# Expert sums in banks of eight keys, neuron weights prepared later in each eight, and turned x tiles spread over the first row quarters

## The reference

```python
def peer(h, w_query, sub_keys, u_emb, v_emb):
    ...
    s_val, s_idx = lax.top_k(s, PEER_TOPK)
    cand = s_val[..., 0, :, None] + s_val[..., 1, None, :]
    ...
    gate = jax.nn.softmax(best, -1).astype(t.dtype)
    ...
        ub = jnp.take(u_emb, eb, axis=0)
        vb = jnp.take(v_emb, eb, axis=0)
        act = jax.nn.gelu(jnp.einsum('td,ted->te', tb, ub), approximate=False) * gb
        return jnp.einsum('te,ted->td', act, vb)
...
    x = x + ga2 * peer(modulate(rmsnorm(x, g_ffn[l]), sh2, sc2), w_query[l], sub_keys[l], u_emb[l], v_emb[l])
return rmsnorm(x, g_final)
```

## Time and profile before

| | |
|---|---|
| three runs | 3451.1, 3449.22, 3443.9 us; median 3449.22 |
| profiled execution | 3447.79 us, its span 3446.0 us |
| PE busy | 98% of the span |
| DVE, POOL, ACT busy | 69%, 52%, 29% |
| V sweep, PE's first to last matmul | 2385.35 to 3430.23 us |

### The profile page before, as it was taken

One profiled execution on the slowest core, in us unless ns is written; L12 is line 12 of the kernel. 1 busy time (PEld: TensorE's weight loads), 2 busy tenths in 40 slices (PEclk: granted clock), 3 DMA queues, 4 the chain that ended last, 5 costly groups with the idle time before them and its releaser, 6 DMA issues.

```text
span 3446.0 us, 44792 instructions
## 1 busy us (share of the span) xinstructions
PE 3373.8 (98%) x16931; PEld 2935.1 (85%) x16931; DVE 2367.3 (69%) x3856; ACT 1008.6 (29%) x1152; POOL 1805.6 (52%) x904
## 2 busy tenths in 40 slices
PE   6999999999999999999999999999999999999998
PEld 3688888766888899999999999999888888888886
DVE  2288886746414759993887798864667776767766
ACT  3332211244123232223222222223233233323233
POOL 1210000213444345676666666666777777778764
PEclk8999999999999999999999999999999999999999
DMA  9655643565423236776677767778988888888872
GB/s 371 257 190 201 220 155 120 184 230 205 161 98 147 90 125 244 265 289 268 266 304 300 290 270 310 307 306 321 377 321 333 318 322 330 316 321 329 320 275 98
DMA packets 184619, 874.72 MB, mean 254 GB/s; under 512 B 16621, under 2 KB 77501, under 8 KB 97844
## 3 DMA queue, kind: packets, MB, share of 16 engines
q1 hardware_dynamic: 122160, 525.38, 41.9%
q0 software_dynamic: 38688, 281.15, 20.2%
q10 hardware_dynamic: 23652, 66.69, 5.1%
HBM read 803.78 MB, written 69.32 MB: 253 GB/s over the span
## 4 chain that ended last, share of the span: by engine, by line
PE 88%; DVE 7%; DMA 2%; POOL 1%; issue 1%; ACT 1%; ACTq 0%; DVEq 0%; SPq 0%; POOLq 0%
PE bank L2096 82%; PE bank L2357 2%; PE bank L2473 1%; DMA ring<-in_w_mod 1%; PE bank L2331 1%; DVE b L1861 1%; POOL low L770 1%; DVE rows_a L1800 1%; DMA low<-in_conv_w 1%; DVE b L1841 0%; PE bank L2104 0%; DVE rows_c L1800 0%; PE bank L2457 0%; DVE tiny L1856 0%; DVE rows_b L1800 0%
## 5 line engine op out<-in xcount | busy, mean ns | idle before, releaser
L812 POOL TENSOR_TENSOR split<-ring,split 128x1024 fp32r<-128x1024 f32 x544 | 1303.6, 2410 | 542.6 <-ACT split L1150 540.4
L2096 PE MATMUL bank<-h_hi,split 128*128 128x384 f32 (+1 forms) x4608 | 1222.0, 341 | 8.2 <-POOL split L812 7.0
L1150 ACT ACTIVATE split<-ring 128x1024 fp32r<-128x1024 f32 x544 | 578.0, 1063 | 1607.0 <-PE bank L2096 1584.9
L2096 PE MATMUL bank<-split,a_split 128*128 128x512 f32 x4608 | 1045.0, 389 | 0.1
L2096 PEld LDWEIGHTS bank<-split,a_split 128*128 128x128 f32 x4608 | 865.0, 188 | 179.8 <-POOL split L812 0.5
L2096 PEld LDWEIGHTS bank<-h_hi,split 128*128 128x128 f32 x4608 | 839.4, 188 | 29.6 <-POOL split L812 8.8
L2096 PE MATMUL bank<-h_lo,split 128*128 128x384 f32 (+1 forms) x2304 | 785.2, 341 | 0.0
L1978 DVE TENSOR_TENSOR acc<-acc,bank 128x512 f32<-128x512 f32 x372 | 251.6, 683 | 289.7 <-PE bank L2096 288.8
L2096 PEld LDWEIGHTS bank<-h_lo,split 128*128 128x128 f32 x2304 | 433.8, 188 | 9.4
L2096 PE MATMUL bank<-hT_hi,w_hi 128*128 128x512 f32 (+1 forms) x768 | 289.8, 377 | 5.4 <-POOL ring_lo L732 2.2
L2096 PE MATMUL bank<-hT_lo,w_hi 128*128 128x512 f32 (+1 forms) x768 | 287.1, 374 | 0.0
(11 more groups left out here) (317 smaller groups left out, 3789.9 us busy)
## 6 DMA issues: line engine op xcount, KB each, us to landing
ring<-in_u_emb SPq DMA_DIRECT2D x128, 1024.0 KB
ring<-in_v_emb SPq DMA_DIRECT2D x128, 1024.0 KB
ring<-in_w_mod SPq DMA_DIRECT2D x48, 1024.0 KB
ring<-in_w_in SPq DMA_DIRECT2D x44, 1024.0 KB
ring<-in_w_mod SPq DMA_DIRECT2D x64, 512.0 KB, 4.5
neurons<-tiny ACTq DMA_DIRECT2D x128, 192.0 KB
gate_table<-b ACTq DMA_DIRECT2D x6, 4096.0 KB, 14.8
weigh<-neurons SPq DMA_DIRECT2D x32, 768.0 KB
```

Source lines behind the costliest of these rows:

```text
L812: nc.gpsimd.tensor_tensor(split[:, r % 2, 1, at].bitcast(F32R), ring[:, r % 4, :, :].rearrange("p k n -> p (k n)")[:, at], split[:, r % 2, ...
L1150: nc.scalar.activation(split[:, q % 2, 0, at].bitcast(F32R), ring[:, q, :, :].rearrange("p k n -> p (k n)")[:, at], ACT.Copy)\
L2096: last = mm(out_, left[a].bitcast(F32R), right[b].bitcast(F32R), start=start and n == 0, stop=stop and n == 2)
```

## The change

Three edits.

1. *Eights.* Units alternate between two groups: unit 8i + k has group 2i + k % 2 and quarter k // 2. Both units of a pair write the same banks, so a bank gathers eight keys and is flushed once in two units. The merges stand in the last eight units.
2. *A group's weights.* SP loads the next two groups in front of v_load(8i + 2) and v_load(8i + 4); in the first eight units in front of v_load(4) and v_load(6). `a_hi` stands in units 6 and 7 of an eight, between the two high halves, and waits for the unit's own matmuls. `weigh_group` stands in units 5 and 6. `rest_group(g + 2)` opens unit 7 and `rest_group(g + 1)` opens the next eight. `add_rows` is left out of unit 7 and made up in the next unit. The second group's weights are made ahead of the sweep. Two small buffers get other places in SBUF.
3. *Start.* PE turns x tiles 0 and 1 in front of quarter n = 4, tile 2 in front of n = 5 and tile 3 in front of n = 7.

```diff
-            def v_load(unit, group, q):
+            def v_load(unit, group, k):
                 sp.wait_ge(split_made, unit * 2 + 2 * (V0 - 3))
...
-                    if k == 2 and not first:
-                        sp.wait_ge(a_split_made, i * 2)
-                        weigh_load(i * 2 + 1, 1)
-                    if k == 6 and not last:
-                        sp.wait_ge(a_split_made, i * 2 + 1)
-                        weigh_load(i * 2 + 2, 0)
-                    v_load(i * 8 + k, i * 2 + k // 4, k % 4)
+                    if k in (2, 4) and not last:
+                        sp.wait_ge(a_split_made, i * 2 + k // 2)
+                        weigh_load(i * 2 + 1 + k // 2, k // 2 - 1)
+                    v_load(i * 8 + k, i * 2 + k % 2, k)
...
             for k in range(4, 8):
-                if k == 6:
-                    sp.wait_ge(a_split_made, 1)
-                    weigh_load(2, 0)
-                v_load(k, 1, k % 4)
+                if k % 2 == 0:
+                    sp.wait_ge(a_split_made, k // 2 - 1)
+                    weigh_load(k // 2, k // 2 - 2)
+                v_load(k, k % 2, k)
...
-            def sweep_unit(unit, q):
-                for h in range(2):
-                    next_hi(unit + NK, q, h)
+            def sweep_unit(unit, q, turn=None):
+                next_hi(unit + NK, q, 0)
+                if turn:
+                    act.wait_ge(split_used, (unit + NK) * 2 + (2 * U0 + 2))
+                    a_hi(*turn)
+                next_hi(unit + NK, q, 1)
...
                 for k in range(8):
-                    sweep_unit(i * 8 + k, k % 4)
-                    if k % 4 == 1:
-                        a_hi((k // 4 + 1) % 2, i * 2 + (k // 4 + 1))
+                    sweep_unit(i * 8 + k, k % 4, (k - 6, i * 2 + (k - 4)) if k > 5 else None)
...
+            def flush_here(unit, j):
+                if unit % 2:
+                    (merge if unit >= NK - 8 else flush)(unit // 2, j)
...
             for unit in range(NK):
-                g = unit // 4
-                flush_here = merge if g == GROUPS - 1 else flush
+                g, k = unit // 8 * 2, unit % 8
+                if k == 7 and g + 2 < GROUPS:
+                    rest_group(g + 2)
+                if k == 0 and g:
+                    rest_group(g + 1)
                 flush_here(unit, 0)
-                if unit % 4 == 0 and g + 1 < GROUPS:
-                    weigh_group(g + 1)
+                if k in (5, 6) and g + 2 < GROUPS:
+                    weigh_group(g + k - 3)
...
-                if unit % 4 == 2 and g + 1 < GROUPS:
-                    rest_group(g + 1)
-                while rows_added < SLOTS and 3 + rows_added - rows_added // 8 <= unit:
+                while k < 7 and rows_added < SLOTS and 3 + rows_added - rows_added // 8 <= unit:
                     add_rows(rows_added)
                     rows_added += 1
...
-                    for t in range(LT):
-                        for g in range(4):
-                            turn_x(t, g)
+                for t in ((0, 1), (2,), (), (3,))[n - 4] if 4 <= n < 8 else ():
+                    for g in range(4):
+                        turn_x(t, g)
...
-                    elif not first or o > 3:
-                        pe.wait_ge(sum_free, unit * JD + (j - 3))
+                    elif s == 0 and (not first or o > 3):
+                        pe.wait_ge(sum_free, i * (4 * JD) + (o - 3))
...
-                                   [split[:, k % 2, h, a * NB:(a + 1) * NB] for h in range(2)], a == 0, a == GROUP - 1)
+                                   [split[:, k % 2, h, a * NB:(a + 1) * NB] for h in range(2)],
+                                   s == 0 and a == 0, s == 1 and a == GROUP - 1)
```

More of the change, by code:

```diff
@@ L294, in hybrid_layer @@
         act_s = small[:, 1792:1920]
+        h2_last = small[:, 1920:2048]
+        nval_last = tiny[:, 2720:2848]
         ga2_part = [small[:, i * NB:(i + 1) * NB] for i in range(3)] + [ga2_last]
@@ L655, in weigh_load, with sweep_loads @@
                   .then_inc(weigh_full[s], 16)
-            def sweep_loads(i, first=False, last=False):
+            def sweep_loads(i, last=False):
                 for k in range(8):
@@ L676, in _ @@
             for k in range(4):
-                v_load(k, 0, k)
+                v_load(k, k % 2, k)
             for b in range(2):
@@ L1308, in _ @@
             for k in range(PRE + CHUNKS * CHUNK_UNITS, NK):
-                if k == NK - 2:
-                    a_hi(0, 0)
+                if k >= NK - 2:
+                    a_hi(k - NK + 2, k - NK + 2)
                 neurons(k, k % 4)
-            def sweep_unit(unit, q):
-                for h in range(2):
-                    next_hi(unit + NK, q, h)
+            def sweep_unit(unit, q, turn=None):
[4 more added lines that the diff above has]
+                next_hi(unit + NK, q, 1)
             for k in range(8):
-                sweep_unit(k, k % 4)
-                if k % 4 == 1:
-                    a_hi((k // 4 + 1) % 2, k // 4 + 1)
+                sweep_unit(k, k % 4, (0, 2) if k == 6 else (1, 3) if k == 7 else None)
                 if k == 0:
@@ L1960, in rest_group, with full_bank, flush, merge @@
                                         a_split[:, g % 2, 0, :, :], ALU.subtract).then_inc(a_split_made, 1)
-            def full_bank(unit, j):
+            def full_bank(pair, j):
                 if j < JD - 1:
-                    dve.wait_ge(sum_full, 2 * unit + j + 1)
+                    dve.wait_ge(sum_full, 2 * pair + j + 1)
                 else:
[L1967 to L1974, removed]
+                    dve.wait_ge(split_used, 2 * (V0 + 2 * pair + 1) + 2)
+                return bank[:, 4 + (JD * pair + j) % 4, :]
+            def flush(pair, j):
+                src = full_bank(pair, j)
+                part = acc[:, j, (pair % 4) * NB:(pair % 4 + 1) * NB]
+                if pair < 4:
                     nc.vector.tensor_copy(part, src).then_inc(sum_free, 1)
                     return
-                dve.wait_ge(sum_free, JD * (unit - 4) + j + 1)
+                dve.wait_ge(sum_free, JD * (pair - 4) + j + 1)
                 nc.vector.tensor_tensor(part, part, src, ALU.add).then_inc(sum_free, 1)
-            def merge(unit, j):
-                q = unit % 4
+            def merge(pair, j):
+                q = pair % 4
                 o = JD * q + j
                 part = acc[:, j, q * NB:(q + 1) * NB]
-                flush(unit, j)
-                dve.wait_ge(sum_free, JD * unit + j + 1)
+                flush(pair, j)
+                dve.wait_ge(sum_free, JD * pair + j + 1)
                 nc.vector.tensor_tensor(part, part, ga2_part[q], ALU.mult).then_inc(merge_step, 1)
@@ L2523, in _, with sums @@
                 neurons(k, k % 4)
-            def sums(unit, k, a_count, first=False):
-                pe.wait_ge(a_split_made, a_count)
-                s = k // 4 % 2
+            def sums(i, k, first=False):
+                unit, s = i * 8 + k, k % 2
+                pe.wait_ge(a_split_made, i * 2 + (s + 1))
                 for j in range(JD):
-                    o = JD * k + j
+                    o = JD * (k // 2) + j
                     if first and o < 2:
@@ L2542, in sums @@
                                    [a_split[:, s, h, a, j * P:(j + 1) * P] for h in range(2)],
-                                   [split[:, k % 2, h, a * NB:(a + 1) * NB] for h in range(2)], a == 0, a == GROUP - 1)
+                                   [split[:, k % 2, h, a * NB:(a + 1) * NB] for h in range(2)],
+                                   s == 0 and a == 0, s == 1 and a == GROUP - 1)
                         if j == JD - 1 and a % 2:
                             last.then_inc(split_used, 1)
-                    if j < JD - 1:
+                    if s == 1 and j < JD - 1:
                         last.then_inc(sum_full, 1)
             for k in range(8):
-                sums(k, k, k // 4 + 1, True)
+                sums(0, k, True)
             with pe.Fori(1, GROUPS // 2) as i:
                 for k in range(8):
-                    sums(i * 8 + k, k, i * 2 + (k // 4 + 1))
+                    sums(i, k)
 _INS = ['x', 'c', 'ctx', 'c_ctx', 'w_mod', 'b_mod', 'g_mix', 'g_ffn', 'w_in', 'w_gate', 'b_gate', 'g_mhn', 'conv_w',
```

13 lines of the change are left out of this document (5 added, 8 removed).

## The result

The changed kernel takes 3467.07 us (median of 6 runs) against 3449.43 before, a ratio of 1.0049 with a 95% interval of 1.0037 to 1.0061. The forecast was 3457 within 3440 to 3468, slower. Its profiled execution took 3469.9 us, with a span of 3468.1.

What follows compares the result with a forecast made beforehand. PE was taken to bound the V sweep, with DVE waiting for it. From 3447.8 us, -3.3 (end), -2.3 (start), +2.5 (unit 4) and +12.3 (six stalls) gave 3457.0 us, 0.27% more; range 3440 to 3468.

Steps and rivals of the forecast that it cites:

- the six places: V sweep, units 17, 25, 33, 73, 81, 89: PE waits for POOL's split, 2.05 us each, +12.3 us.
- the loads: V sweep: weigh loads ahead of v loads on SP's queue; +2.5 us at unit 4, 0 in steady state.
- the start: Input stage: quarter n = 4 multiplied earlier, so its ring place's refill lands near 44.1; -2.3 us, between 0 and -5.1.
- the clock: Rival, chance 0.13: PE's clock halves for 3.4 us behind each of six stalls, +10 us, total 3467.
- E: V sweep: end of unit 15, from which the links delaying unit 17's split are timed.
- Short `rest_group`: Units 16, 24, 32, 72, 80, 88: it takes 1.75 us because POOL stands; longer would make 3.65 a place.
- Unit 4: Start of V sweep: 1.57 MB ahead of v_load(4) delays it to 2416; +2.5 us, between 0 and +14.
- the rival's delay of 18.7 us and stall of 14: Rival, chance 0.07: SP's queue stays slow at the sweep's start, v_load(4) lands at 2427.7, total 3469.
- The loads of units 8i + 2: V sweep: loads behind weigh loads on SP need 12 to 15 us of 17.6 available; hidden, 0.
- The end: Last units: merges spread over eight units leave DVE ready for the last bank's flush; -3.3 us, at most -3.4.
- Not slower, as a rival: Rival, chance 0.17: POOL's wait stays hidden, six stalls vanish, 3442.2; with the start's full 5.1 us 3439.4, chance 0.10.
- row 13: Unit 16: the deferred row that POOL's gather of row 16 awaits; forecast added 5.6 us after unit 15's end.

Runs made afterwards that it cites:

- all loads later: Changed kernel with SP's weigh loads moved later, in the first eight units and in the steady state; sweep 1059.5 us, ratio to before 1.0025.
- the gather later alone: Changed kernel with POOL's gathers behind an eight's first unit moved one unit on, SP's loads unmoved; sweep 1054.2 us, ratio to before 1.0004.
- all three: Changed kernel with the left-out row ahead of the second `rest_group`, and first and steady weigh loads later; sweep 1058.9 us, ratio to before 1.0033.
- row first: Changed kernel with the row left out of unit 7 added ahead of the second `rest_group`; sweep 1067.8 us, ratio to before 1.0050.
- row in unit 7: Changed kernel with first and steady weigh loads later and `add_rows` no longer left out of unit 7; sweep 1051.1 us, ratio to before 1.0003.
- gather later: Changed kernel with first and steady weigh loads later and POOL's gathers behind an eight's first unit moved one on; sweep 1045.1 us, ratio 0.9975.

## Why the prediction held, and where it was off

*The total.* 3467.1 lies 10.1 above the forecast of 3457.0, outside the 3452 to 3462 that I gave the forecast alone, and 0.9 below the upper end of the range. By terms: 1.6 is the distance of the medians from the profiled execution, 2.9 the six places (15.2 instead of 12.3), 3.3 the loads (5.8 instead of 2.5) and 2.3 the start, which the totals don't show. The upper end, 3468, was drawn to take in the clock falling at six places, and that did not come. So the mechanism was right, and that the range held was in part luck.

*The six places.* Right in place, number and mechanism. The mis-sized term is the price: 2.05 forecast, 2.4 measured (14.4 for six, all loads later). The chain shows where it lies. I counted `a_hi` from E, the start of the next unit's matmuls. This row is unit 16's first:

```profile
2526.37 0.39 PE L2097 MATMUL bank<-split,a_split 128*128 128x512 f32 x1
```

`a_hi` began at 2526.64, 0.27 later, behind the modelled end of unit 15's last matmul (2526.54). The other links fitted: 1.5, 1.7, 2.36, 0.26, 0.94 and 2.36 a half. PE began half 1 of unit 17 at 2538.19, E + 11.8 instead of E + 11.6. Behind each of the two waits PE's first two matmuls stand 0.33 us apart instead of 0.23 (2535.86 and 2536.19), which makes up the rest.

*Short `rest_group`.* I took 1.75 and not 3.3 for these places because POOL stands. That was right (1.67 net in the chain). What I failed to ask is what a remedy would do: as soon as POOL no longer stands, `rest_group` collides.

*Unit 4.* +2.5 forecast, in two pieces; the wait came in one piece of 3.2, and about 1.4 of clock behind it. (At the lower clock PE needed 2.7 us for half 0 instead of 1.36, so half 1 was in time.) These two rows of SP and ACT answer to the earlier trace rows:

```profile
2401.02 9.50 SPq L645 DMA_DIRECT2D ring<-in_v_emb  x2
2421.83 2.00 ACT L1147 ACTIVATE split<-ring 128x1024 fp32r<-128x1024 f32 x2 [14.56 <-DMA ring<-in_v_emb]
```

From the sweep's start the load landed 32.2 us on instead of 23.9, so 1.57 MB ahead of it cost 8.3 us, 7 in the forecast. That is 0.19 MB/us, between the two rates from which I chose (0.41 and 1.05/12.5 = 0.08). It is nearer to the lower one than I thought, and far from the rival's delay of 18.7 us and stall of 14.

*The loads of units 8i + 2.* Forecast 0, hidden. In the steady state that held, but not in the first eight: SP issued unit 10's load at 2457.26 and ACT had it 15.2 later, and unit 10 lost 1.2. These rows are the DMA engines' window ahead of it, the first and last of five loads that ACT issues there, and ACT's waits for the loads of units 10 and 18.

```profile
2446.70:2451.00 4.30, 4.30 (x21) 1.00 0.00 0
2451.67 0.34 ACTq L1331 DMA_DIRECT2D g_final_row<-in_g_final  x1
2453.84 1.14 ACTq L1333 DMA_DIRECT2D ga_last<-mod_rows  x1
2472.45 2.01 ACT L1147 ACTIVATE split<-ring 128x1024 fp32r<-128x1024 f32 x2 [10.27 <-DMA ring<-in_v_emb]
2534.02 2.00 ACT L1147 ACTIVATE split<-ring 128x1024 fp32r<-128x1024 f32 x2 [4.94 <-DMA ring<-in_v_emb]
```

From 2446.7 to 2451 the engines stand, so nothing was left over from unit 4. Then ACT issues 2.1 MB just ahead of SP's weigh loads, once in the sweep (1024 KB for the final norm and four loads of 256 KB). From the end of the `rest_group` that releases SP to ACT's rounding it took 17.0 us at unit 10, where 16.9 were left (this `rest_group` ended 4.1 us into unit 7, not 3.4). At unit 18 it took 11.8, and 10.1 to 12.6 in the later eights where ACT waits at this place, so my 12 to 15 were if anything high for those. The step that failed is the count of the bytes: it left out ACT's 2.1 MB. With the gathers moved ("the gather later alone") the same stretch took 14.1 us at unit 10 and 9.5 to 10.3 later, again 4 to 5 apart. That ACT's loads make this difference is argued from the rows; no run moved them. With the weigh loads moved later ACT waits once instead of 28 times.

*The clock.* As a rival it asked for a fall behind each of the six. There it stayed 1.00 (2535 to 2540). It fell behind the longer single wait at unit 4, to 0.69, as it had behind one of the two 2.24 us waits of before. The experiments are as mixed: behind a wait of 2.60 us in front of unit 33 it was 0.72 in "all three" and 1.00 in "row first". Part of the rival's mechanism came, at another place.

*The end.* -3.3 forecast, 15.8 to 12.45 measured, in every version with the eights. Halved flushes brought nothing else, as forecast: DVE's waits for PE at the flushes grew from 289 to 331 us.

*The start.* -2.3 forecast; 1.5 to 1.9 at the first refills, about 1.7 near 159 us over all profiles, 0.4 in this one. The 41.6 from which the forecast counts stands in no row.

*Not slower, as a rival.* It needed row 13 by E + 3.5. It came at E + 5.8 (2532.20), so POOL's wait of 6.9 to 8.6 us could not hide.

## What to carry to other kernels

When work on one engine is put off by a step, look for what another engine has queued behind its wait for that work. Here a gather that was in no hurry stood in front of a split that was, and moving the gather behind the split was worth 14.4 us with the loads out of the way (11.8 without), more than the edit's whole gain. And a load moved ahead in a queue is paid for by the load behind it, at the rate which that queue gets beside the others: here 8.3 us for 1.57 MB.

## What was not expected of the hardware

A DVE subtraction of two SBUF tiles lasted 1.75 us alone. Where it became ready while POOL subtracted two SBUF tiles in two halves back to back, it lasted 4.65 to 6.44 and ended 1.6 behind POOL's second half ("all three" and "row in unit 7"). Where POOL had stood 0.40 us between its halves, the subtraction got in between them and lasted 2.21, and POOL's second half took 3.47 us instead of 2.42 ("gather later"). An indirect DMA's issue on POOL lasted 2.3 us instead of 0.96 when that subtraction was running, and ended 0.8 behind it.
